# Five openings multiplied block by block of the contraction, with both halves of the weights at once

## The reference

```
for layer in range(DEPTH):                       # first network, DEPTH = 2
    x = x + 0.5 * swiglu(rms_norm(x, ffn_norm[layer, 0]), ...)
    h = rms_norm(x, mix_norm[layer])
    x = x + (parallel_attention_mixer(h, ...) if layer % 2 == 0 else rwkv7_time_mix(h, ...))
    x = x + 0.5 * swiglu(rms_norm(x, ffn_norm[layer, 1]), ...)
for layer in range(DEPTH):                       # second network: x and the context xc
    h  = modulate(rms_norm_2(x,  g_norm1[layer]), sh1, sc1)
    hc = modulate(rms_norm_2(xc, g_norm1[layer]), csh1, csc1)
    glu, gate, (qm, km, vm), (qg, kg, vg) = project_tokens(h, ...)     # z = h @ w_in
    glu_c, gate_c, (qmc, kmc, vmc), (qgc, kgc, vgc) = project_tokens(hc, ...)
    x = x + g1 * merge_branches(glu, gate, o_m, o_g, ...)
    x = x + g2 * conv_ffn(modulate(rms_norm_2(x, g_norm2[layer]), sh2, sc2), ...)
    # layer 0 only: the same two steps for xc; in layer 1 only keys and values of xc are needed
```

## Time and profile before

| | us |
|---|---|
| median of three runs | 2568.14 |
| lowest and highest of them | 2568.07, 2571.44 |
| the profiled execution | 2569.5 |
| its span, first to last instruction | 2567.7 |
| PE, DVE, ACT busy in the span | 2531.5, 2063.9, 1292.2 |
| PE waits of 0.7 us or more behind its start at 11.37 us | 13, the longest 1.19 |
| weights and other data read from HBM | 451.49 MB, 176 GB/s |

### The profile page before, as it was taken

One profiled execution on the slowest core, in us unless ns is written; L12 is line 12 of the kernel. 1 busy time (PEld: TensorE's weight loads), 2 busy tenths in 40 slices (PEclk: granted clock), 3 DMA queues, 4 the chain that ended last, 5 costly groups with the idle time before them and its releaser, 6 DMA issues.

```text
span 2567.7 us, 49796 instructions
## 1 busy us (share of the span) xinstructions
PE 2531.5 (99%) x20096; PEld 2356.2 (92%) x20096; DVE 2063.9 (80%) x3076; ACT 1292.2 (50%) x1778; POOL 52.4 (2%) x68
## 2 busy tenths in 40 slices
PE   8999999999999999999999999999999999999999
PEld 8998799999988899998979999885999988859999
DVE  7986589889877489967887876797888877978877
ACT  5345554353363453355565445546554465465543
POOL 0000000000011000000000000000000000000000
PEclk9999999999999999999999999999999999999999
DMA  7764267667622067753424555340355444404553
GB/s 294 281 242 166 98 231 285 237 262 277 231 101 106 26 258 265 258 195 133 165 83 174 186 187 190 132 165 6 142 198 194 181 153 143 165 2 147 197 184 143
DMA packets 61518, 454.60 MB, mean 177 GB/s; under 512 B 6872, under 2 KB 6896, under 8 KB 9280
## 3 DMA queue, kind: packets, MB, share of 16 engines
q1 hardware_dynamic: 54720, 394.24, 42.8%
q0 software_dynamic: 6656, 58.35, 5.8%
HBM read 451.49 MB, written 1.07 MB: 176 GB/s over the span
## 4 chain that ended last, share of the span: by engine, by line
PE 85%; DVE 9%; ACT 4%; issue 1%; DMA 0%; DVEq 0%; SPq 0%; ACTq 0%
PE ps L823 20%; PE ps L655 15%; PE ps L656 15%; PE ps L657 15%; PE ps L1117 3%; PE ps L1553 2%; DVE w_parts L2399 1%; PE ps L1412 1%; DVE half_parts L2604 1%; PE ps L1570 1%; PE ps L597 1%; PE ps L1587 1%; ACT half_parts L1847 1%; PE ps L1480 1%; PE ps L1424 1%
## 5 line engine op out<-in xcount | busy, mean ns | idle before, releaser
L1760 ACT ACTIVATE w_parts<-ring 128x1024 fp32r<-128x1024 f32 x462 | 463.2, 1052 | 348.1 <-PE ps L655 347.6
L655 PE MATMUL ps<-normed_parts,w_parts 128*128 128x256 f32 x2160 | 603.9, 280 | 1.6 <-DVE w_parts L2399 1.6
L656 PE MATMUL ps<-normed_parts,w_parts 128*128 128x256 f32 x2160 | 603.1, 279 | 0.0
L657 PE MATMUL ps<-normed_parts,w_parts 128*128 128x256 f32 x2160 | 602.4, 279 | 0.0
L2399 DVE SCALAR_TENSOR_TENSOR w_parts<-ring,w_parts 128x1024 fp32r<-128x1024 f32 x462 | 544.6, 1220 | 18.9 <-ACT w_parts L1760 18.2
L823 PE MATMUL ps<-stream_high,half_parts 128*128 128x256 f32 x2288 | 437.3, 287 | 3.2 <-DVE half_parts L2604 2.3
L655 PEld LDWEIGHTS ps<-normed_parts,w_parts 128*128 128x128 f32 x2160 | 405.9, 188 | 2.3 <-DVE w_parts L2399 2.3
L656 PEld LDWEIGHTS ps<-normed_parts,w_parts 128*128 128x128 f32 x2160 | 406.0, 188 | 0.0
L657 PEld LDWEIGHTS ps<-normed_parts,w_parts 128*128 128x128 f32 x2160 | 406.0, 188 | 0.0
L2604 DVE SCALAR_TENSOR_TENSOR half_parts<-ring,half_parts 128x1024 fp32r<-128x1024 f32 x233 | 281.6, 1214 | 117.4 <-ACT half_parts L1847 116.7
L823 PEld LDWEIGHTS ps<-stream_high,half_parts 128*128 128x128 f32 x2288 | 358.3, 188 | 9.5 <-issue 7.9
(11 more groups left out here) (504 smaller groups left out, 3829.0 us busy)
## 6 DMA issues: line engine op xcount, KB each, us to landing
ring<-in_weights SPq DMA_DIRECT2D x373, 1024.0 KB, 4.8
arena<-in_mod_weights POOLq DMA_DIRECT2D x32, 1536.0 KB, 6.7
arena<-in_cond POOLq DMA_DIRECT2D x8, 512.0 KB, 6.2
arena<-toeplitz_rows POOLq DMA_DIRECT2D x1, 1536.0 KB, 10.7
x<-in_x SPq DMA_DIRECT2D x1, 1024.0 KB, 5.0
arena<-in_ctx POOLq DMA_DIRECT2D x1, 1024.0 KB, 9.6
out<-x SPq DMA_DIRECT2D x4, 256.0 KB, 2.6
arena<-in_rope POOLq DMA_DIRECT2D x1, 640.0 KB, 12.2
```

The lines of the kernel that those rows point to most:

```text
L655: first = pe.matmul(into, wh, high, start=start, stop=False, skip_group_check=True)
L656: pe.matmul(into, wh, low, start=False, stop=False, skip_group_check=True)
L657: return first, pe.matmul(into, wl, high, start=False, stop=stop, skip_group_check=True)
L1760: a(w_parts[:, to, 0, cols], ring[:, at, cols], ACT.Copy).then_inc(s["w_high"], 1)
```

## The change

In `split_opening` both halves, m = 0 and m = 1, are taken at the top, so that PE waits there for the low parts of both. Then, for each k, four products stand in a row: high and low weights of m = 0, high and low weights of m = 1, all against the high part of h. The 16 products against the low part of h stand last, again with m innermost. The three single fillers between quarters of the attention's opening are left out. The first `half_used` is marked at the second product of the opening, and the second at the last product that reads the first half, the last but one of the opening. Two column blocks of one bank now share one `start` flag.

```diff
--- before.py
+++ after.py
@@ -859,26 +859,29 @@
 
             def split_opening(i, filler=True):
 
-                for m in range(2):
-                    into = ps[:, mm_n[0] % 4, m * S:(m + 1) * S]
-                    if m == 0:
-                        free_bank()
-                    blocks = [split_block() for _ in range(KT)]
-                    for k, (high, low, opens) in enumerate(blocks):
-                        if m == 0 and k % 2 == 0:
-                            if filler:
-                                warm((mm_n[0] + 2) % 4, 1 if k else 8)
-                            pe.wait_ge(s["stream_h_high"], QUARTERS * i + k // 2 + 1)
-                        mm = pe.matmul(into, high, stream_high[:, k, :], start=(k == 0), stop=False, skip_group_check=True)
+                free_bank()
+                into = [ps[:, mm_n[0] % 4, m * S:(m + 1) * S] for m in range(2)]
+                blocks = [[split_block() for _ in range(KT)] for _ in range(2)]
+                for k in range(KT):
+                    if k % 2 == 0:
+                        if filler and k == 0:
+                            warm((mm_n[0] + 2) % 4, 8)
+                        pe.wait_ge(s["stream_h_high"], QUARTERS * i + k // 2 + 1)
+                    for m in range(2):
+                        high, low, opens = blocks[m][k]
+                        mm = pe.matmul(into[m], high, stream_high[:, k, :], start=(k == m == 0), stop=False, skip_group_check=True)
                         w.used(mm)
-                    for k, (high, low, opens) in enumerate(blocks):
-                        mm = pe.matmul(into, low, stream_high[:, k, :], start=False, stop=False, skip_group_check=True)
-                        if opens:
+                        mm = pe.matmul(into[m], low, stream_high[:, k, :], start=False, stop=False, skip_group_check=True)
+                        if m == k == 0:
                             mm.then_inc(s["half_used"], 1)
-                    for k, (high, low, opens) in enumerate(blocks):
-                        if m == 0 and k % 2 == 0:
-                            pe.wait_ge(s["stream_h_low"], QUARTERS * i + k // 2 + 1)
-                        mm = pe.matmul(into, high, stream_low[:, k, :], start=False, stop=(k == KT - 1), skip_group_check=True)
+                for k in range(KT):
+                    if k % 2 == 0:
+                        pe.wait_ge(s["stream_h_low"], QUARTERS * i + k // 2 + 1)
+                    for m in range(2):
+                        high, low, opens = blocks[m][k]
+                        mm = pe.matmul(into[m], high, stream_low[:, k, :], start=False, stop=(k == KT - 1), skip_group_check=True)
+                        if k == KT - 1 and m == 0:
+                            mm.then_inc(s["half_used"], 1)
                 mm.then_inc(s["mm_ready"], 1)
                 mm_n[0] += 1
```

## The result

| | us |
|---|---|
| before, median of 17 runs (lowest, highest) | 2569.61 (2567.69, 2573.53) |
| after, median of 17 runs (lowest, highest) | 2573.2 (2569.28, 2580.82) |
| ratio, with its 95% interval | 1.0018 (1.0011 to 1.0026) |
| span of the profiled execution after | 2578.6 |

A forecast was written before the change was run, and what follows sets the result against it. PE was taken to bound the kernel, busy 2531.5 of 2567.7 us. Terms -1.43 - 0.10 + 1.40 + 2.75 gave +2.6 us, so 2570.7 us on the median of 2568.14; range 2568.3 to 2573.8.

The forecast's parts named there:

- attention's opening: Attention's opening: PE no longer stops at later quarters and half 2 limits the end; a gain of 1.43 us.
- openings of streams 0 to 2: Streams 0, 1, 2, the opening itself: 48 products stay at 0.1167 us, only small stops go; 0.1 us gained.
- half 3 of streams 0 and 1: Behind these openings: half 3 is released 1.63 us later but still in time, no stop; rival of late halves, chance 0.14.
- half 4 of stream 2: Stream 2: the later half 3 pushes the work queued on DVE and ACT, so half 4 comes late; loss 1.40 us.
- stream 3's opening, without the clock: Stream 3's opening: PE stops 3.77 us at the top for half 1's low part, which DVE makes last; loss 2.75 us.
- The clock falls in stream 3's stop: Rival: PE's rest ahead of stream 3's opening lowers the clock; 2.6 us on top, 2573.3 us; chance 0.14.
- products of 0.21 us and more behind the stop: Sign: products this slow behind stream 3's stop would break the prediction.
- I keep the gain whole: Behind the attention's opening: waits hang on PE's own results, so all 1.43 us stay; bounds 0 and 1.78.
- its slack of 0.10 us: Half 3 in streams 0, 1, 2: ready 2.93 us after product 47 starts, wanted after 3.03 us; no stop.
- absorbed: Rival: quicker ACT or DVE work, or the chain to stream 3, hides stream 2's 1.4 us; 2569.3 us, chance 0.12.
- stops at quarters in the old opening: Stream 3's opening before the change: 1.02 us of stops, all at quarters of `stream_high` that ACT is still writing.
- The wait that doesn't bind: Rival: half 1's low part is early in stream 3 too; 2567.0 us, or 2565.6 without stream 2's loss; chance 0.03.

## Why the prediction was wrong

It called the change a slowdown of 0.1% that a measurement can't tell from none, and gave the bound of 0.2% a chance of 0.12. The time lies inside the range, but the ratio of 1.0018 is clear of one, and it makes 4.6 us of loss where the sum has 2.6. By its steps:

| step | predicted, us | measured, us |
|---|---|---|
| attention's opening | -1.43 | -1.53 by its own length, -1.38 at the next network |
| openings of streams 0 to 2 | -0.10 | -0.03 to -0.08 in streams 0 and 1; stream 2's 0.05 is in its row below |
| half 3 of streams 0 and 1 | 0 | 0 |
| half 4 of stream 2 | +1.40 | +1.36 |
| stream 3's opening, without the clock | +2.75 | +2.95 |
| the clock in stream 3's opening | 0, or +2.6 at 0.14 | +1.55 in 32 of 41 executions |
| sum | +2.6 | +4.4 with the fall, +2.9 without |

**The step that failed** is "The clock falls in stream 3's stop", "Chance 0.14". The sum put this term at nothing. The mechanism of that rival and its place were right; its likelihood was not. I set the rest of 3.8 us against the start's 11.37 us and the 1.19 us of the kernel's other waits and took it for nearer to the latter. In three of four executions it was enough, and there the sum lacks 1.55 us. The prediction had named products of 0.21 us and more behind the stop as a sign against it, and they came. The size was off the other way: priced from the start, where the slow stretch was longer, it was 2.6 us; here the clock was down for 3.4 us, and 1.55 were lost.

**The call itself**, no change that can be told, failed for a second reason: its bound of 5.1 us was for few runs. With 17 on each side the interval is 2 us each way, and even the 2.9 us without the fall, or the 2.6 of the sum, lie outside it. A forecast of +0.1% should have said that its own centre was a loss.

**The attention**: right, by half 2 as forecast: the products of the last part end near 212.9 and the wait for half 2 is 0.1 us. "I keep the gain whole" held nearly: of the opening's 1.53 us, 0.15 to 0.4 are gone at the next network, in the six traces with the new order.

**Half 3**: its slack of 0.10 us held in all traces, in streams 0, 1 and 2. It was a close call.

**Stream 2**: right to 0.04 us, by the queue behind the late half, and the chain to stream 3 hid none of it. The rival "absorbed" is out.

**Stream 3's stop**: right in cause (one DVE row moved ahead removes it) and in size to 0.2 us; 0.1 us of the remainder lies in the stop and 0.08 in the opening, which takes 5.68 us after it, not 5.60. One reading was wrong without touching the sum: of the 1.02 us called stops at quarters in the old opening, 0.40 are the gap behind its first product, which is not such a stop.

**The wait that doesn't bind** was out as expected.

## What to carry to other kernels

When several inputs are waited for at the top of a block instead of each at its first use, look for the one that the producer makes last: here a half that nothing had needed until halfway became a stop of 3.9 us from start to start, and one moved line on DVE turned stream 3's loss into a gain. A mark that frees a buffer, moved back, delays more than the buffer's next user: follow the released engine's queue, where a residual update and four squares stood behind it and the delay came out at the next half. And price PE's rest with the clock in it: where a stop as long as this one can't be removed, a few products that nobody needs, sized by their measured time, saved 1.5 us here by the local time.

## What the runs showed of the hardware

**A stretch of 20.5 us at half clock, now and then.** In stream 0's head loop, where PE does many small products, some executions run at 0.5. The windows of after, and of before in the same place:

```profile
1292.00:1313.00 21.00, 21.00 (x66) 0.52 0.00 1
```

```profile
1290.00:1310.00 20.00, 18.14 (x108) 1.00 0.00 1
```

It costs 8.3 us, shows as a mean clock of 0.996, and came in 14 of 104 executions of the kernel before in the three comparisons, and in 12 of the 13 sets of runs of changed kernels, 32 of 159. The counts don't set these two shares apart. It makes the upper end of nearly every kernel's times. Why it comes in one execution and not in the next isn't settled.

**Two paces in the long loops.** Within a feed-forward network the products start either 116.7 or 117.8 ns apart, for nearly the whole network and at full granted clock, and which one it is changes from trace to trace. The windows show it as 852 or 860 products in 100 us; first before, then after, near the end of the kernel:

```profile
2440.00:2540.00 100.00, 100.00 (x852) 1.00 0.52 188
```

```profile
2450.00:2550.00 100.00, 100.00 (x860) 1.00 0.52 187
```

The slow pace costs 1.5 us a network. The program has seven networks, and in the fourteen traces none to four of them are slow, so up to 6 us between two traces come from this alone. That it makes most of the spread from 2567 to 2574 us of one kernel fits, but no kernel has more than two traces. What sets it wasn't tried.

**A float32 product that nobody reads isn't cheap.** A 128x256 product in plain float32 took 0.44 us (12.25 us for 28), one of the rounded kind 0.117.
